# First attention of a two-block transformer kernel: where the probabilities are divided by their row sums, and how TensorE turns them

## What is computed

```python
def one_block(qblk):
    s = jnp.einsum('bqkgd,bskd->bkgqs', qblk, k).astype(jnp.float32)
    p = jax.nn.softmax(s, axis=-1).astype(v.dtype)
    return jnp.einsum('bkgqs,bskd->bqkgd', p, v)

o = lax.map(one_block, qb)
```

## Time and profile before

| | |
|---|---|
| median of three runs | 2630.74 us |
| profiled execution, first to last instruction (span) | 2631.7 us |
| mean granted TensorE clock | 0.965 of 2.4 GHz |
| PE busy | 2435.6 us, 93%, 12094 instructions |
| PEld busy | 2045.6 us, 78% |
| DVE busy | 1163.6 us, 44% |
| ACT busy | 854.4 us, 32% |
| POOL busy | 764.2 us, 29% |
| turning products of the first attention, L698 | first start 238.7 us, last start 484.6 us |

### The profile page before, as it was taken

One profiled execution on the slowest core, in us unless ns is written; L12 is line 12 of the kernel. 1 busy time (PEld: TensorE's weight loads), 2 busy tenths in 40 slices (PEclk: granted clock), 3 DMA queues, 4 the chain that ended last, 5 costly groups with the idle time before them and its releaser, 6 DMA issues.

```text
span 2631.7 us, 32586 instructions
## 1 busy us (share of the span) xinstructions
PE 2435.6 (93%) x12094; PEld 2045.6 (78%) x12094; DVE 1163.6 (44%) x1376; ACT 854.4 (32%) x1137; POOL 764.2 (29%) x667
## 2 busy tenths in 40 slices
PE   2797999887999999999978989889999999999997
PEld 2686888776888888888767888879778888888885
DVE  7766888685442344234453351625221121222234
ACT  3225777314221122124444343434112111112221
POOL 3343222241333333333312111020223333333331
PEclk8897999998999999999988999999999999999998
DMA  5310000550111111111121101101001111111131
GB/s 222 137 66 34 25 16 25 216 208 32 48 48 48 48 48 48 48 58 50 38 95 59 61 27 50 52 16 62 32 28 48 48 48 52 48 48 40 48 120 72
DMA packets 45708, 165.49 MB, mean 63 GB/s; under 512 B 4048, under 2 KB 5840, under 8 KB 44496
## 3 DMA queue, kind: packets, MB, share of 16 engines
q1 hardware_dynamic: 45648, 164.67, 17.7%
HBM read 156.26 MB, written 8.39 MB: 63 GB/s over the span
## 4 chain that ended last, share of the span: by engine, by line
PE 83%; DVE 9%; ACT 4%; issue 2%; DMA 1%; POOL 0%; DVEq 0%; SPq 0%; ACTq 0%; POOLq 0%
PE acc L597 63%; PE bank L833 3%; PE turn L820 3%; PE turn L698 2%; PE bank L712 2%; DVE ADA L1290 2%; PE acc L681 2%; PE bank L698 1%; PE acc L806 1%; PE bank L588 1%; DVE K2L L1629 1%; DMA XT<-in_xT 1%; PE turn L615 1%; PE bank L876 1%; DVE K2L L1630 1%
## 5 line engine op out<-in xcount | busy, mean ns | idle before, releaser
L597 PE MATMUL acc<-HH,WH 128*128 128x512 f32 x1888 | 592.1, 395 | 50.5 <-POOL HL L508 29.5
L597 PE MATMUL acc<-HL,WH 128*128 128x512 f32 x1888 | 585.4, 391 | 0.0
L597 PE MATMUL acc<-HH,WL 128*128 128x512 f32 x1888 | 584.7, 391 | 0.0
L495 POOL TENSOR_TENSOR WH<-WF,CON 128x16 fp32r<-128x16 f32 x186 | 53.6, 288 | 1576.8 <-PE acc L597 1437.2
L597 PEld LDWEIGHTS acc<-HH,WH 128*128 128x128 f32 x1888 | 354.5, 189 | 134.3 <-POOL HL L508 25.9
L498 POOL TENSOR_TENSOR WL<-WF,WH 128x1024 fp32r<-128x1024 f32 (+2 forms) x186 | 439.4, 2362 | 15.5
L597 PEld LDWEIGHTS acc<-HL,WH 128*128 128x128 f32 x1888 | 357.7, 189 | 75.2
L597 PEld LDWEIGHTS acc<-HH,WL 128*128 128x128 f32 x1888 | 356.5, 189 | 75.0
L1542 DVE SCALAR_TENSOR_TENSOR CV<-EV,VEC,CV 128x1023 f32<-128x1023 f32 x44 | 105.5, 2397 | 242.4 <-ACT CV L1093 242.4
L1489 DVE TENSOR_TENSOR XT<-XT,EV 128x1024 f32 (+1 forms) x40 | 98.0, 2451 | 209.1 <-ACT EV L1074 209.1
L496 POOL TENSOR_SCALAR WH<-WF 128x1008 fp32r<-128x1008 f32 (+2 forms) x186 | 190.3, 1023 | 0.0
(11 more groups left out here) (293 smaller groups left out, 3701.5 us busy)
## 6 DMA issues: line engine op xcount, KB each, us to landing
WF<-in_w SPq DMA_DIRECT2D x150, 512.0 KB, 3.2
ADA<-in_ada SPq DMA_DIRECT2D x13, 2048.0 KB, 15.6
BIAS<-in_bias SPq DMA_DIRECT2D x8, 1152.0 KB, 5.1
ADA<-in_ada SPq DMA_DIRECT2D x6, 1024.0 KB, 4.9
WF<-in_w SPq DMA_DIRECT2D x24, 256.0 KB, 2.6
XT<-in_xT SPq DMA_DIRECT2D x2, 2048.0 KB, 13.0
ADA<-in_ada SPq DMA_DIRECT2D x8, 512.0 KB, 3.3
XT<-in_xT SPq DMA_DIRECT2D x8, 512.0 KB, 16.9
```

The costliest lines, as they stand in the source:

```text
L495: pool.tensor_tensor(h[:, 0:FEW], f[:, 0:FEW], zero.to_broadcast([P, FEW]), ALU.add).then_inc(w_hi, 1)
L597: last = pe.matmul(acc[:, slot, HALF * c:HALF * c + HALF], w[slot][:, k, :], x[:, k, HALF * c:HALF * c + HALF], start=(k == 0 and w is WH ...
```

## The change

GpSimd no longer makes a diagonal. It multiplies all 1024 columns of `EX[u % 4]` by `RC`, in place, with two instructions: a `tensor_tensor` over the first 16 columns and a `tensor_scalar` with a per-row scalar over the other 1008. TensorE then turns `EX` with `transpose` (the identity is the other operand) in place of the products with `DG`. The semaphore, now `exn_ready`, counts two steps a unit, and the waits on it are doubled. Nothing else moves; `DG` stays in use in the second attention, where VectorE makes it.

```diff
-            def diagonal(it, u):
+            def normalise(it, u):

                 pool.wait_ge(rc_ready, it * 16 + (u + 1))
-                pool.tensor_tensor(DG[u % 2][:, :], ident, RC[:, u % 2:u % 2 + 1].to_broadcast([P, P]), ALU.mult
-                                   ).then_inc(dga_ready, 1)
+                x, r = EX[u % 4], RC[:, u % 2:u % 2 + 1]
+                pool.tensor_tensor(x[:, 0:FEW], x[:, 0:FEW], r.to_broadcast([P, FEW]), ALU.mult).then_inc(exn_ready, 1)
+                pool.tensor_scalar(x[:, FEW:], x[:, FEW:], r, None, ALU.mult).then_inc(exn_ready, 1)
...
-                    pe.wait_ge(dga_ready, it * 16 + (u + 1))
+                    pe.wait_ge(exn_ready, it * 32 + (2 * u + 2))
...
-                            mm = pe.matmul(turns[q % 3][:, P * (k % 4):P * (k % 4) + P], EX[u % 4][:, P * k:P * k + P], DG[u % 2][:, :],
-                                           start=True, stop=True)
+                            mm = pe.transpose(turns[q % 3][:, P * (k % 4):P * (k % 4) + P], EX[u % 4][:, P * k:P * k + P], ident)
```

More of the change, by code:

```diff
@@ L280, in build @@
         qh_ready, qst_act, qst_pool = sem("qh_ready"), sem("qst_act"), sem("qst_pool")
-        scores_done, nb_ready, exp_done, rc_ready, dga_ready = (
-            sem("scores_done"), sem("nb_ready"), sem("exp_done"), sem("rc_ready"), sem("dga_ready"))
+        scores_done, nb_ready, exp_done, rc_ready, exn_ready = (
+            sem("scores_done"), sem("nb_ready"), sem("exp_done"), sem("rc_ready"), sem("exn_ready"))
         pt_done, pth_ready, ptl_ready, pv_done, otmp_ready, o_ready, mh_ready, ml_ready = (
@@ L520, in stack_queries @@
                     if done is not None:
-                        pool.wait_ge(dga_ready, done)
+                        pool.wait_ge(exn_ready, done)
                     dst = QST[s % 2][64:128, :, :].rearrange("p (i j) q -> p i j q", j=2)[:, :, b, :]
@@ L536, in attend @@
                     if u < 15 or not last:
-                        diagonal(it, u + 1)
+                        normalise(it, u + 1)
                     if 1 <= u <= 3:
-                        stack_queries(it, 1, u - 1, it * 16 + (u + 2))
+                        stack_queries(it, 1, u - 1, it * 32 + (2 * u + 4))
                     if 9 <= u <= 11 and not last:
-                        stack_queries(it, 2, u - 9, it * 16 + (u + 2))
+                        stack_queries(it, 2, u - 9, it * 32 + (2 * u + 4))
                     if u == 8:
@@ L556, in _ @@
                 stack_queries(0, 0, step)
-            diagonal(0, 0)
+            normalise(0, 0)
             with steps.loop(3, 2) as it:
```

## The result

The changed kernel takes 2667.37 us (median of four runs, 2666.34 to 2668.24) for 2631.03 of the kernel before, timed beside it: a ratio of 1.0139, with a 95% interval of 1.0124 to 1.0153. The forecast was 2614. The profiled execution has a span of 2665.9 us.

A forecast was written before the change was run, and what follows sets the result against it. TensorE was taken as the bound, with a three-engine loop just below; 12.0 (ordinary pairs) + 2.3 (gather) + 2.4 (u = 8) - 0.3 (seams) + about 0.3 (start) made 16.7 us, giving 2614, range 2602 to 2629.

The forecast's parts named there:

- GpSimd's part: First attention: the 0.40 us diagonal goes, a multiplication taken as 1.3 us comes; hidden in pairs, not at the seam.
- rival 2: GpSimd becomes the bound in the attention: with a 3.5 us multiplication 262 us for 246, kernel 2646; chance 0.04.
- 4.2 + N: Time in us of the two-unit loop through GpSimd's multiplication, N being its length; said to decide from N = 3.3.
- at u = 8: Interval where NBI waits for ML: from 8.50 to 7.9 us, four times 0.6, 2.4 us in all.
- rival 1: TensorE's clock falls in attention pauses: seams up to 14 us, typically 2621; five pairs or more lost, chance 0.07.
- The case of the Trainium skill: Transposes not counting as work for the clock: all 32 attention pairs at half clock, kernel about 2750; chance 0.02.
- The seam's term: Between two `it`, TensorE waits for the multiplication: interval 9.33 + 0.1, three seams giving -0.3 us.
- Two sums of the clock's rival: Attention pairs at half clock: ten give 2645; all 32 give 368 us for 240, about 2750.
- TensorE's part: Turning a unit in the attention falls from 1.70 to 0.86 us, 54 us of TensorE's work over 64 units.
- the loop afterwards: The chain through TensorE, VectorE and ScalarE then holds an ordinary attention pair at 6.73 us, not 5.75.
- With a gather: Pairs with `gather_o` in the unit (u = 4 and 12): 7.19 us, eight times 0.29, 2.3 us in all.
- the wait that takes its place: TensorE stands about 1 us in each ordinary attention pair, waiting for `PTL`.

The follow-up runs named there:

- the kernel with constants: The changed kernel with the per-row scalar of GpSimd's wide multiplication replaced by the constants 1.0 and 1.0, two operations: 2619.45 us, ratio 0.9956.
- TensorE's half alone: The kernel before with transposes in place of TensorE's products with the diagonal, which GpSimd still makes; no division by row sums: 2616.41 us, ratio 0.9948.

## Why the prediction was wrong

**The step that failed** is the price of the new instruction in "GpSimd's part": "I take 1.3: one source and the same 1008 columns". It was 0.22 + 2.80 = 3.02 us. The row it came from the earlier trace rows is of an instruction with two operations, the changed one has one. The diff said so (`r, None`), and I called both a multiplication over 1008 columns and looked for reasons in the operand and in contention. The bound from the other side, 3.5 from the earlier trace rows, did hold the true value; the choice within the bounds was wrong, and the chance of 0.04 for a long multiplication was far too small for an instruction of which the trace had no example.

**The second failure** is the point of decision in rival 2: "It decides from N = 3.3 on". That is where the loop reaches the old pair of 7.48; it passes the forecast's own 6.73 from N = 2.5 on. By 4.2 + N a pair at N = 3.02 is 7.2 us, still below 7.48. The loop was about right for pairs with nothing else in GpSimd's queue: 7.43 and 7.29 behind u = 9 and u = 11 of the last `it`, at 1.00. But six units of sixteen have a stacking instruction there, and then 3.02 + 1.04 and more stand in a row for each unit; the earlier trace rows's `ML` is a seventh and an eighth case. I had spread them as 0.6 us a unit over all units, and a mean hides exactly the units that get late. The two kernels that differ in this length alone, 2619.45 and 2667.37, show it: over one `it`, from the start at 321.32, the pairs with stacking or behind it lose 1.4 to 3.0 us (8.75 for 7.36, 9.71 for 6.73, 8.75 for 6.72, 9.22 for 7.26), the one behind u = 13 1.0 (7.72 for 6.73), the seam 2.1 (12.58 for 10.47), the one at u = 8 nothing (7.74 for 7.81). The pair behind the seam loses nothing either (7.61 for 7.62), but only because the shorter kernel was itself at 0.85 there; behind the next seam, where it kept 1.00, it is 7.60 for 6.62. The last `it` stacks nothing at u = 9 to 11, and there the changed kernel takes 7.43 for the 8.75 to 10.07 of the three others. The averaging failed at a shorter length too: for 2.16 the prediction gave 2618, and the two-source multiplication with 2.09 took 2644.49.

**The clock**, rival 1, came too, on top: 0.87 in the window shown above, where TensorE has a pause of about 2 us in most pairs. It makes TensorE's work 12.7 us longer than in the kernel with constants; how much of the 31.1 us of idle time follows from that is not separated. The same pair shows its price: behind u = 3 it takes 8.75 at 1.00 in one `it` and 9.86 at 0.83 in another. In the kernels with a short multiplication it falls at the seams or just behind them, at the lowest to a mean of 0.77 over the interval, and costs 0.5 to about 2 us for a seam and the pair behind it; in most of them it falls once more before the last values (0.74 or 0.75); the prediction had named this place and up to 4.8 us. The case of the Trainium skill ("TensorE: Matmul & The Clock Gate", Part 4), full speed not engaging for transposes, did not happen: in the kernel with TensorE's half alone, ordinary pairs of 6.73 us, with 16 transposes each, ran at 1.00.

**The seam's term** was short as well. It was 9.43 for a multiplication of 1.3 us. With 0.22 + 1.03 the kernel with constants has seams of 9.81 to 10.79, each with a pause of TensorE of 3.36 us and at 0.79 to 0.93.

**Two sums of the clock's rival** do not come out: ten pairs at half clock are 2614 + 48 = 2662, not 2645, and 368 us for 240 give 2759, not about 2750. Neither changes the forecast.

**What was right.** TensorE's part and the loop afterwards: 6.73 us forecast and measured (6.63 in the last `it`), and term by term: in the pair shown above `PTL`, the maximum, `PTL` of T(o) and the values start 1.27, 2.48, 3.97 and 4.71 us after the end of the values before, for 1.26, 2.48, 3.98 and 4.72. With a gather it is 7.16 to 7.36 for 7.19, at u = 8 7.8 for 7.9. The claim that TensorE's saving of 54 us gives only some 17 at the end holds (14.5 measured with this half alone), and so does the wait that takes its place, `PTL`, with 0.8 us on average for about 1. Had the multiplication taken what I priced, the kernel would have been at 2619.45, which the version with constants shows, inside the range and 5 us above the forecast. Over the 30 intervals of the sum it is 4.3 us longer: 2.8 at the three seams and 1.6 in the pairs behind two of them, where the clock was 0.85 and 0.87.

## What to carry to other kernels

Before an instruction's duration is borrowed from a row, compare the whole form: the operation count and which operand is absent, not only engine, type and size. On GpSimd here, giving a `tensor_scalar` a second operation by 1.0 made it 2.5 times as fast. And where an engine's queue carries occasional work, test the new length in the units that have it; averaged over all units it looks harmless.

## What was not expected of the hardware

- GpSimd, `tensor_scalar`, 1008 columns of float32 in place: one operation 2.73 us (constant) or 2.80 (per-row scalar), two operations 1.03 or 1.11. A two-source multiplication by a broadcast column took 1.87, where two full sources of 1024 columns take 2.46 us on average between 640 and 1000 us of the kernel before (L498).
- The slow form did not hold up VectorE: `NBI` ran in 0.16 us beside it (330.73, above). Beside the two-source form VectorE's 1.22 us product took 2.09, and beside the form with two operations 1.35 on average in one piece and 1.58 in halves.
- Two operations with the multiplication in halves: 0.68 us for 496 and 0.69 for 512 columns, for 1.11 in one piece, so a second instruction costs 0.26 us and brings the release 0.4 us forward.
